# Three of eight chunk pairs of gate and up by Strassen's seven products, in ten feed-forward panels

## The reference

```python
a = rmsnorm(h, g_mix);  z = a @ w_in          # q, k, v, cv, cg
h = h + concat([dilated_attention(q, k, v), conformer_conv(cv, cg)]) @ w_out
f = rmsnorm(h, g_ffn)
h = h + (silu(f @ w_gate) * (f @ w_up)) @ w_down      # the part that the change is in
h = h + (p @ w_ple) * sigmoid(rmsnorm(h, g_ple) @ w_pgate + b_pgate)
return rmsnorm(h, g_final)
```

## Time and profile before

| | |
|---|---|
| median of 3 runs | 1186.91 us (1186.88 to 1187.06) |
| the profiled execution | 1187.32 us, of which the span of the trace is 1185.5 us |
| PE, PE weight load | 1173.7 us, 992.0 us busy in the span |
| DVE, ACT, POOL | 723.8, 554.6, 111.0 us busy |
| mean DMA rate | 188 GB/s |

### The profile page before, as it was taken

The page is one execution under the profiler, slowest core; times in us unless marked ns, Lnnn a source line. Parts: engine busy times, 40 slices in busy tenths (PEclk is TensorE's granted clock), DMA queues, the critical chain, the costliest instruction groups (busy, mean ns, idle before and its releaser), DMA issues.

```text
span 1185.5 us, 15597 instructions
## 1 busy us (share of the span) xinstructions
PE 1173.7 (99%) x5734; PEld 992.0 (84%) x5734; DVE 723.8 (61%) x965; ACT 554.6 (47%) x699; POOL 111.0 (9%) x66
## 2 busy tenths in 40 slices
PE   9999999999999999999999999999999999999996
PEld 8889989988888888888888888888888888888886
DVE  6589757768664556464646555464646555567674
ACT  6544465456554434444343434434443434456552
POOL 0212454344000000000000000000000000000111
PEclk9999999999999999999999999999999999999999
DMA  9655555545557555565555555655656555554541
GB/s 343 203 181 178 186 168 178 177 143 177 189 187 263 177 198 192 180 208 178 192 197 180 189 198 178 202 186 185 205 177 199 190 180 196 191 180 176 188 167 71
DMA packets 111703, 223.25 MB, mean 188 GB/s; under 512 B 3786, under 2 KB 5010, under 8 KB 111409
## 3 DMA queue, kind: packets, MB, share of 16 engines
q1 hardware_dynamic: 111200, 222.08, 56.3%
q10 hardware_dynamic: 464, 0.66, 0.2%
HBM read 220.63 MB, written 2.10 MB: 188 GB/s over the span
## 4 chain that ended last, share of the span: by engine, by line
PE 93%; issue 1%; ACT 1%; DVE 1%; DMA 1%; POOL 1%; SPq 0%; POOLq 0%; DVEq 0%; ACTq 0%
PE ps L1105 27%; PE ps L1103 27%; PE ps L1104 27%; PE ps L1135 3%; PE ps L1136 3%; PE ps L1137 3%; PE ps L1145 1%; DMA arena<-in_p 1%; ACT w_hi L492 1%; ACT nT_hi L524 0%; PE ps L1112 0%; PE ps L1292 0%; DVE w_lo L749 0%; PE ps L1360 0%; PE ps L1362 0%
## 5 line engine op out<-in xcount | busy, mean ns | idle before, releaser
L749 DVE TENSOR_TENSOR w_lo<-w_raw,w_hi 128x1024 fp32r<-128x1024 f32 x370 | 458.7, 1241 | 431.3 <-ACT w_hi L492 431.1
L492 ACT ACTIVATE w_hi<-w_raw 128x1024 fp32r<-128x1024 f32 x406 | 430.2, 1060 | 587.2 <-PE ps L1105 531.4
L1103 PE MATMUL ps<-w_hi,nT_hi 128*128 128x512 f32 x984 | 386.3, 393 | 0.0
L1105 PE MATMUL ps<-w_hi,nT_lo 128*128 128x512 f32 x984 | 383.2, 389 | 0.0
L1104 PE MATMUL ps<-w_lo,nT_hi 128*128 128x512 f32 x984 | 382.9, 389 | 0.0
L1105 PEld LDWEIGHTS ps<-w_hi,nT_lo 128*128 128x128 f32 x984 | 184.7, 188 | 38.7
L1104 PEld LDWEIGHTS ps<-w_lo,nT_hi 128*128 128x128 f32 x984 | 184.8, 188 | 37.7
L1103 PEld LDWEIGHTS ps<-w_hi,nT_hi 128*128 128x128 f32 x984 | 184.8, 188 | 37.7
L1103 PE MATMUL ps<-w_hi,oT_hi 128*128 128x512 f32 x480 | 187.9, 392 | 0.0
L1105 PE MATMUL ps<-w_hi,oT_lo 128*128 128x512 f32 x480 | 186.9, 389 | 0.0
L1104 PE MATMUL ps<-w_lo,oT_hi 128*128 128x512 f32 x480 | 186.8, 389 | 0.0
(11 more groups left out here) (164 smaller groups left out, 598.0 us busy)
## 6 DMA issues: line engine op xcount, KB each, us to landing
w_raw<-in_w_gate SPq DMA_DIRECT2D x44, 1024.0 KB, 5.1
w_raw<-in_w_up SPq DMA_DIRECT2D x44, 1024.0 KB, 5.1
w_raw<-in_w_down SPq DMA_DIRECT2D x44, 1024.0 KB, 5.0
w_raw<-in_w_in SPq DMA_DIRECT2D x32, 1024.0 KB, 5.1
w_raw<-in_w_out SPq DMA_DIRECT2D x16, 1024.0 KB, 5.0
w_raw<-in_w_pgate SPq DMA_DIRECT2D x16, 1024.0 KB, 5.0
w_raw<-in_w_in SPq DMA_DIRECT2D x14, 512.0 KB, 9.9
w_raw<-in_w_ple SPq DMA_DIRECT2D x2, 1024.0 KB, 5.4
```

The costliest lines, as they stand in the source:

```text
L492: nc.scalar.activation(slot_of(m)[0], w_raw[:, (m // 2) % RAW, rows], ACT.Copy).then_inc(hi_ready, 1)
L749: nc.vector.tensor_tensor(lo, w_raw[:, (m // 2) % RAW, rows], hi.bitcast(F32), ALU.subtract).then_inc(lo_ready, 1)
L1103: nc.tensor.matmul(banks[t][:, :], x_hi[:, k, rows], w_hi[:, s, k], start=start, stop=False)
L1105: ins = nc.tensor.matmul(banks[t][:, :], x_lo[:, k, rows], w_hi[:, s, k], start=False, stop=stop)
```

## The change

With two chunks k of x and of the weights and two token tiles t, gate and up together are a 2 x 2 product of blocks: x[t, k] times W[k, gate or up]. In the ten panels of the loop, chunk pairs 0, 3 and 5 ("S" in `QUAD_KINDS`) are computed with seven block products in the Strassen-Winograd form, the other five ("P") with eight, accumulated into the same banks. The sums of x (four per S pair) are formed once, before the loop, on POOL; the sums of weights are three DVE subtractions per S pair and panel (one 128 x 1024, two 128 x 512). For this x is scaled by rstd before the loop (POOL joins hi and lo, DVE scales, ACT and DVE split again), and the first panel (FFN0) takes gate and up in the same units, one chunk at a time. An S pair has four units, of 6, 3, 6 and 6 matmuls (2, 1, 2, 2 weight tiles); a P pair has two units of 12. A panel now has 30 units, a split runs six units ahead in six slots. Gate, up and the four banks of pure products are put together by DVE and ACT at the end of the pairs: two ACT copies, eight DVE combinations, silu of an SBUF tile, two DVE products. The act transposes go to banks `SPARE` and `P4`, the down columns to the banks of P1, P5 and P7, P6. The last panel of the loop is written out behind it. The bias and final gain rows are loaded after the loop instead of ahead of it.

The core of the diff (the products' banks, the sources, the lists of DVE, ACT and PE for a panel):

```diff
+QUAD_KINDS = "SPPSPSPP"
+QUAD_UNITS = [4 if kind == "S" else 2 for kind in QUAD_KINDS]
+QUAD_AT = [sum(QUAD_UNITS[:i]) for i in range(QUADS + 1)]
+DOWN_AT = QUAD_AT[QUADS]
+PER_LOOP = DOWN_AT + 8
+LOOP_SLOTS = 6
...
+        P1, P2, P3, P4, P5, P6, P7, SPARE = ps[2], ps[3], ps[4], ps[6], ps[5], ps[1], ps[0], ps[7]
+        DOWN_BANKS = [(P1, P5), (P7, P6), (P1, P5), (P7, P6)]
+        ACT_BANKS = (SPARE, P4)
...
+            if kind == "S":
+                return (raw[:, 0:4:3], raw[:, 2:3], w_sum[:, 0:2], w_sum[:, 2:4])[unit]
...
+            elif in_loop(m) and m >= LOOP0 + LOOP_SLOTS:
+                engine.wait_ge(half_done, m - LOOP_SLOTS + 1 + PER_LOOP * it)
...
 SP
+                sp.dma_start(raw[:, 0:4:3], w_gate_v[:, 2 * i:2 * i + 2, cols]).then_inc(quad_ready[i % RAW], 16)
+                sp.dma_start(raw[:, 1:3], w_up_v[:, 2 * i:2 * i + 2, cols]).then_inc(quad_ready[i % RAW], 16)
...
+            sp.wait_ge(half_done, PLE0)
             sp.dma_start(b_rows, b_pgate[0].partition_broadcast(P)).then_inc(rows_loaded, 16)
             sp.dma_start(gf_rows, g_final.partition_broadcast(P)).then_inc(rows_loaded, 16)
...
 POOL
+            for i in range(6):
+                join_x(i)
             root(1, 2)
+            for i in range(6, QUADS):
+                join_x(i)
+            for n, i in enumerate(S_QUADS):
+                x_sums(n, i)
...
 ACT, behind the first panel and then step t of a panel
+            swish_of(LOOP0)
+            for m in range(LOOP0 + SLOTS, LOOP0 + LOOP_SLOTS):
+                split_hi(m)
...
+                    if t == 2:
+                        act_hi(ACT_BANKS, it)
+                    if t == QUAD_AT[S_LAST + 1]:
+                        sc.wait_ge(half_done, LOOP0 + t + PER_LOOP * it)
+                        nc.scalar.activation(p1_sum, P1[:, :], ACT.Copy).then_inc(product_copied, 1)
+                        nc.scalar.activation(p5_sum, P5[:, :], ACT.Copy).then_inc(product_copied, 1)
+                    if t == DOWN_AT:
+                        sc.wait_ge(combined, 3 + 8 * it)
+                        nc.scalar.activation(swish[:, 0], swish[:, 0], ACT.Silu).then_inc(swish_ready, 1)
+                    if t == DOWN_AT + 2:
+                        sc.wait_ge(combined, 5 + 8 * it)
+                        nc.scalar.activation(swish[:, 1], swish[:, 1], ACT.Silu).then_inc(swish_ready, 1)
+                    m = LOOP0 + t + LOOP_SLOTS
+                    if not last or t + LOOP_SLOTS < PER_LOOP:
+                        split_hi(m, it)
...
 DVE, weight_sums(at, e, i, it): at 0, then at 1
+                    nc.vector.tensor_tensor(w_sum[:, 0:2], raw[:, 1:3], raw[:, 0:2], ALU.subtract).then_inc(w_sum_ready, 1)
...
+                    nc.vector.tensor_tensor(w_sum[:, 2], raw[:, 2], w_sum[:, 0], ALU.subtract).then_inc(w_sum_ready, 1)
+                    ve.wait_ge(w_sum_ready, 3 * n + 2 + done)
+                    nc.vector.tensor_tensor(w_sum[:, 3], raw[:, 3], w_sum[:, 2], ALU.subtract).then_inc(w_sum_ready, 1)
...
 DVE, step t of a panel
+                    if t == 2:
+                        act_lo(ACT_BANKS, it)
+                    if t == QUAD_AT[S_LAST + 1] + 1:
+                        ve.wait_ge(product_copied, 2 + 2 * it)
+                        combine(u2_sum, p1_sum, P6[:, :])
+                        ve.wait_ge(combined, 1 + 8 * it)
+                        combine(u3_sum, u2_sum, P7[:, :])
+                    if t == DOWN_AT:
+                        ve.wait_ge(half_done, LOOP0 + t + PER_LOOP * it)
+                        combine(swish[:, 0], p1_sum, P2[:, :])
+                        ve.wait_ge(combined, 3 + 8 * it)
+                        combine(p1_sum, p5_sum, P3[:, :])
+                        combine(swish[:, 1], u3_sum, P4[:, :])
+                        combine(act[:, 1], u3_sum, SPARE[:, :])
+                    if t == DOWN_AT + 1:
+                        ve.wait_ge(combined, 6 + 8 * it)
+                        combine(act[:, 0], u2_sum, p1_sum)
+                        combine(act[:, 1], act[:, 1], p5_sum)
+                    if t == DOWN_AT + 3:
+                        ve.wait_ge(combined, 8 + 8 * it)
+                        ve.wait_ge(swish_ready, 4 + 2 * it)
+                        for tile in range(TT):
+                            ins = nc.vector.tensor_tensor(act[:, tile], act[:, tile], swish[:, tile], ALU.mult)
+                        ins.then_inc(act_ready, 1)
+                    if t in (DOWN_AT + 2, DOWN_AT + 4, DOWN_AT + 6):
+                        add_down((t - DOWN_AT) // 2 - 1, it)
+                    for i in S_QUADS:
+                        ahead = QUAD_AT[i] - LOOP_SLOTS
+                        if ahead >= 0 and t in (ahead, ahead + 1):
+                            weight_sums(t - ahead, 0, i, it)
+                        if ahead < 0 and not last and t - PER_LOOP in (ahead, ahead + 1):
+                            weight_sums(t - PER_LOOP - ahead, 1, i, it)
+                    m = LOOP0 + t + LOOP_SLOTS
+                    if not last or t + LOOP_SLOTS < PER_LOOP:
+                        split_lo(m, it)
...
+                add_down(3, it)
...
 PE, seven_products(i, it)
+                block_product(P1, x_block(i, 0, 0), unit_tile(at, 0), first, last)
+                block_product(P2, x_block(i, 0, 1), unit_tile(at, 1), first, False).then_inc(half_done, 1)
+                arrived(at + 1, it)
+                block_product(P3, s4, unit_tile(at + 1, 0), first, False).then_inc(half_done, 1)
+                if first:
+                    turn_act(ACT_BANKS, it)
+                arrived(at + 2, it)
+                block_product(P5, s1, unit_tile(at + 2, 0), first, last)
+                if first:
+                    pe.wait_ge(swish_ready, 1 + 2 * it)
+                    pe.wait_ge(down_read, 7 + 8 * it)
+                block_product(P7, s3, unit_tile(at + 2, 1), first, last).then_inc(half_done, 1)
+                arrived(at + 3, it)
+                if first:
+                    pe.wait_ge(swish_ready, 2 + 2 * it)
+                    pe.wait_ge(down_read, 8 + 8 * it)
+                block_product(P6, s2, unit_tile(at + 3, 0), first, last)
+                if first:
+                    pe.wait_ge(actT_ready, it + 1)
+                block_product(P4, x_block(i, 1, 1), unit_tile(at + 3, 1), first, False).then_inc(half_done, 1)
...
 PE, down column c
+                    if c >= 2:
+                        pe.wait_ge(down_read, 8 + 2 * (c - 1) + 8 * it)
```

More of the change, by code:

```diff
@@ L76 @@
 WARM_UPS = (6, 1, 3)
+RB1_AT = FFN0 + 6
+NORMAL_AT = [RB1_AT + 1 + i // 2 for i in range(QUADS)]
+A_AT = [max(RB1_AT + 2 + i, FFN0 + 2 * i + 3) for i in range(QUADS - 1)] + [LOOP0 - 1]
+S_AT = {i: RB1_AT + 4 + n for n, i in enumerate(S_QUADS)}
 RAW = 4
@@ L977, in _, with feed_forward @@
+                if m in (LOOP0 - SLOTS, LOOP0 - SLOTS + 1):
+                    weight_sums(m - LOOP0 + SLOTS, 0, 0)
                 if not by_pool(m + AHEAD):
                     split_lo(m + AHEAD)
-            swiglu(0, LOOP0)
-            with ve.Fori(0, LOOPS) as it:
+            ve.wait_ge(panel_read, Q_DOWN)
+            first_swiglu()
+            for m in range(LOOP0 + SLOTS, LOOP0 + LOOP_SLOTS):
+                split_lo(m)
+            def feed_forward(it, last):
                 for t in range(PER_LOOP):
@@ L1280, in turn_last, with turn_act, gate_and_up @@
                 turn_h(2, c, LOW[0])
-            def turn_act(j):
+            def turn_act(banks, j):
                 pe.wait_ge(act_ready, j + 1)
-                pe.wait_ge(panel_read, Q_DOWN - 1 + 4 * j)
-                turn(act, 0, HIGH[0]).then_inc(actT_turned, 1)
+                turn(act, 0, banks).then_inc(actT_turned, 1)
+            def gate_and_up(m):
+                arrived(m)
+                s = m % SLOTS
+                i, k = divmod(m - FFN0, 2)
+                for f in range(2):
+                    for t in range(TT):
+                        dst = (LOW[0], HIGH[1])[(f + k) % 2][t][:, :]
+                        row, tok = 2 * i + k, slice(t * P, (t + 1) * P)
+                        nc.tensor.matmul(dst, nT_hi[:, row, tok], w_hi[:, s, f], start=row == 0, stop=False)
+                        nc.tensor.matmul(dst, nT_hi[:, row, tok], w_lo[:, s, f], start=False, stop=False)
+                        ins = nc.tensor.matmul(dst, nT_lo[:, row, tok], w_hi[:, s, f], start=False, stop=row == KC - 1)
+                ins.then_inc(half_done, 1)
@@ new lines, in eight_products @@
+            def eight_products(i, it):
+                at = LOOP0 + QUAD_AT[i]
+                pe.wait_ge(a_ready, i + 1)
+                for k in range(2):
+                    arrived(at + k, it)
+                    for f in range(2):
+                        up = f != k
+                        for t in range(TT):
+                            bank = ((P2, P4), (P3, SPARE))[up][t]
+                            first = up and t == 1 and k == 0 and i == P_FIRST
```

(2 more changed lines are left out.)

374 lines of the change are left out of this document (276 added, 98 removed).

## The result

| kernel | median us | lowest to highest | profiled execution (span) |
|---|---|---|---|
| before | 1186.91 | 1186.59 to 1187.21, 6 runs | 1187.32 (1185.5) |
| after | 1213.62 | 1211.89 to 1214.2, 6 runs | 1212.25 (1210.4) |

The ratio is 1.0222 [1.0209, 1.0235]: slower, as forecast, but by 2.2% instead of 0.8%, and beyond the end of the range at 1208. Between the profiled executions the sum should have come to +9.6 and came to +24.9.

A forecast was written before the change was run, and what follows sets the result against it. PE was taken as the bound. On the profiled execution, -20.4 + 21.6 + 2.24 + 1.8 + 3.1 + 1.0 + 0.3 = +9.6; forecast 1197 us, own range 1192 to 1203, wider range 1188 to 1208.

The forecast's parts named there:

- PE is the bound: Feed-forward loop: it goes at PE's pace, so PE work saved is time saved; a panel without stall takes 64.14 us.
- -20.4: Ten panels: 90 matmuls fewer at 0.2267 us each, a saving of 20.4 us.
- Place one: Panel start: bank P4 is released late because act_lo stands late in DVE's queue; 2.70 us stall, 2.24 in the tenth panel.
- the turn: DVE's queue at the panel's start: the turn of the loop costs 0.46 us.
- Rival C: Loop panels: PE's pauses bring 3 to 4 us at half clock, +15 to +20, 1212 to 1217 us; chance 0.06.
- First panel: First panel: late act transposes (+1.8 us) and a stall before P4 (+3.1 us).
- The wait before the transposes: First panel: transposes due at 2.04 start at 3.86, since the silu of both tiles comes late; +1.8 us.
- Joining and scaling x lies beside sixteen units of PE: Before the loop: this work is hidden; row scale there at about 357, asked for by PE at 361.5.
- The stall before P4: First panel: P4 due at 6.80, act_lo done only at 9.9; +3.1 us.
- Place two: Banks of third and fourth down column: DVE done at 16.29, PE wants them at 16.32; 0.1 a panel, +1.0 us.
- Hidden work: Splits inside Strassen pairs, ACT, weight loads, and joining and scaling x were taken to cost PE no time.
- six slots too few: Splits running ahead: six slots suffice; PE waits for w_lo of a unit would prove them too few.

The follow-up runs named there:

- e8: e7 with the two DVE products that make act two steps later, behind add_down(1); 1170.05 us, 0.9853 of before.
- e2: The changed kernel with nine fp32 matmuls of a zero block added in the pause before P4 in each panel; 1204.9 us, 1.0149 of before.
- e4: The changed kernel with act_hi one step earlier on ACT and act_lo two steps earlier on DVE; 1188.34 us, 1.0007 of before.
- e5: The changed kernel with three more unused DVE additions of 384 columns ahead of act_lo in each panel; 1237.91 us, 1.0427 of before.
- e7: e6 plus the 32-byte pad of e3 and, in the first panel, act_hi one step and act_lo two steps earlier; 1172.73 us, 0.9878 of before.
- e6: e1 with the splits of the third pair's x sums and chunk pairs 6 and 7 moved into the first panel; 1180.8 us, 0.9944 of before.
- e1: The changed kernel with act transposes before the last two down units, their copies right after, first panel written out; 1182.28 us, 0.9957 of before.
- e3: The changed kernel with 32 bytes ahead of the shared buffer, so w_more and a_last start at a multiple of 128; 1211.11 us, 1.0196 of before.
- e9: e7 with 96 bytes of pad instead of 32, so w_more starts 64 bytes past a multiple of 128; 1177.7 us, 0.9918 of before.

## Why the prediction was right in its sign and wrong in its size

- **PE is the bound, and its work goes at full price: right.** -20.4 stands; e8 reaches the panel of 64.14 to 0.01.
- **Place one: right in place, mechanism and order, mis-sized upwards.** 2.22 for 2.70. The ledger without the turn gave 2.24. The 0.46 came from a gap of before, read as the turn's price, although the row itself put 0.39 of it down to ACT and the prediction's own working left 0.09 behind the input. It was worth 8 x 0.46 = 3.7 us too much, and hid part of the error on the other side.
- **Rival C was given 0.06, and held in five panels of nine.** This is the step that failed first: the sum has no term for the clock, and "no other pause above 1.1 is in this trace" stood beside a chance of 0.06, where it only meant that before could not tell. It cost +7.9 in the profiled execution, the largest of the missing terms; without it the kernel would have come to about 1205.7, inside the range. Its mechanism is shown: fillers in the pause take the spells away (e2), a pause of 0.58 has none (e4), one of 3.63 has them in all nine panels (e5). Its size was right for one panel (1.5 to 2 forecast, 1.57 found), wrong in that not every panel has one. The Trainium skill, TensorE: Matmul & The Clock Gate, section on HAM oscillation, has such a loop with waits of about 3 to 5 us. The trace agrees on the kind of loss and shows it at shorter pauses: 2.2 us in a loop of 67 us were followed by half speed in five and in eight of nine panels. The prediction had left open whether its pauses were long enough; at 2.2 us they were, in some panels.
- **First panel: +8.6 instead of +4.9, mis-sized.** The wait before the transposes was forecast at 1.8 and is 3.82. The step took the queues as empty at the panel's start; in truth ACT and DVE come to it late, having stood behind GpSimd's sums of x. "Joining and scaling x lies beside sixteen units of PE" looked at the time when PE asks, not at ACT standing in line. The stall before P4 shrank in exchange from 3.1 to 0.43, a half-clock spell of some 2.0 came in, and two waits for `w_lo`, 0.43 and 0.81. The Trainium skill, SBUF — State Buffer, section on the two separate sides, says that a GpSimd instruction and a DVE one with two SBUF inputs exclude each other for one whole instruction. The two timelines fit such an exclusion, but the price is that of the whole row: 4.25 and 7.74 us for 0.46, over five and more DVE instructions that follow without a gap. No run took the row away, so the exclusion is read from these two and not tested.
- **Place two: right**, +1.3 for +1.0. The dead heat of 16.29 against 16.32 came out as 0.13 a panel. In e7, where `add_down(3)` and `act_lo` stand elsewhere, it was 0.27, and moving two products by two steps removed it (e8).
- **The alignment was missed altogether**, +5.1. That the two new tiles land 96 bytes off could have been seen from the sizes of the allocations. No row of before shows the price, since none of its fp32r matmuls read such a tile.
- **Hidden work: right in the nine later panels.** There PE never waits for `w_lo`, and the weight loads in halves cost nothing that shows. In the first panel it waited twice, behind ACT's and DVE's backlog; by the prediction that would prove six slots too few, but e6, with the same six slots and less work ahead of the panel, has neither wait.

The sign is no luck: without the spells and the alignment, which the sum lacked, the account would stand at +11.9. That it would stand so near +9.6 is in part luck, since 3.8 too much on place one hid 3.7 too little in the first panel.

Not settled: why at one length of pause some panels get a spell and others don't, and the 0.15 a panel that the account lacks. e1 and e8 lose at most 0.05 of these 0.15, so they belong to the pause or to what surrounds it.

## What to carry to other kernels

Where one engine is the bound, write out the queue of each engine that feeds it from the last boundary on, and move the instruction with someone waiting ahead of those with slack: the same 904 us of DVE work gave 1213.6 or 1170.1, of which 5 are the alignment. Price a pause on TensorE as the pause and a possible spell at half clock behind it, and if the pause can't be moved, cheap matmuls in it are worth trying. And after a change in the allocations, look where the tiles that TensorE reads start.

## What the runs showed of the hardware

- An fp32r matmul of 512 columns that reads a tile starting 96 or 64 bytes past a multiple of 128, be it the weights (`w_more`) or the rows of x (`a_last`), takes 0.230 to 0.234 us, aligned 0.2267. The start was the only edit in e3, and the only one between e7 and e9, which ran on different chips.
- Pauses of TensorE and half-clock spells behind them, in nine panels of 64 to 68 us of gapless work each: 0.58 us, none; 2.2 us, in five and in eight; 3.63 us, in all nine. In the first panels of e7, e8 and e9 one pause of 2.3 us was followed by one each time; in e6 2.3 us were not, 2.6 were.
- A GpSimd instruction that reads SBUF took 4.25 and 7.74 us instead of 0.46 beside a gapless row of DVE instructions with two SBUF sources, and ended about 0.3 us after DVE first stood idle.
